# Another order of work around the paired down projections of a two-layer hybrid decoder

## The chip, the cores and the metric

One core of a Trainium2 chip runs the whole kernel in one launch. The metric is the device time of that launch in microseconds. The engines are TensorE (PE in the profile, with its weight loads as PEld), VectorE (DVE), ScalarE (ACT), GpSimd (POOL) and SyncE (SP, which only issues transfers here).

## What is computed

A decoder trunk of two layers over 1024 positions of width 1024, in float32. Each layer adds a mixer (attention heads and a short convolution) and then a gated feed-forward network; the change is in the latter:

```python
def conv_glu_ffn(h, w_up, conv_w, w_down):
    gu = h @ w_up
    g, u = jnp.split(gu, 2, axis=-1)
    g = causal_dwconv(g, conv_w)          # three taps per channel
    return (jax.nn.silu(g) * u) @ w_down  # D_FF = 2816 hidden channels

for layer in range(DEPTH):
    ...
    hn = rms_norm(h, norm_ffn_g[layer])
    h = h + conv_glu_ffn(hn, w_up[layer], conv_ffn_w[layer], w_down[layer])
```

## The kernel before

The residual h lies in SBUF as 8 rows of 128 channels by 1024 positions. The 2816 hidden channels are 22 tiles of 128, f = 0 to 21. Every matmul is made of three passes over float32 values split in a high and a low part (w_hi with hi, w_hi with lo, w_lo with hi), each 128 x 128 by 512 columns.

**Products.** One tile's gates and ups are made from seven block products in place of eight, with sums of quarters of the input (B11, B21, B22, and T1 to T4) and sums of quarters of the weights (A11, A12, A22, and S1 to S4). A product is 12 matmuls into one of four banks, in the order of STEADY: A11 with B11 into bank 0, A22 with T4 into 1, S1 with T1 into 2, S2 with T2 into 3, S3 with T3 into 0, A12 with B21 into 3, S4 with B22 into 2. VectorE puts the products together (`combine`: seven operations named `add_product`), and then adds two taps of the convolution to k_next (`convolve_gates`, one `scalar_tensor_tensor` of 128x1024 each), of which ScalarE has written the middle tap (`center`). ScalarE takes silu and VectorE multiplies by the ups (`value`); the result, k_next, is the tile's hidden value.

**Down projection.** The tiles are taken in pairs; pair p holds the values of tiles 2p and 2p+1. Its down projection is made of seven block products too, each of four rows of 3 matmuls (`down_row`): part one (PART_A) runs A11 with B11 into the four CHAINED banks 4 to 7 and S1 with T1 into the four SINGLE banks 0, 1, 3, 2, as soon as the even tile's value is there. Part two (PART_B) runs S2 with T2 into the CHAINED banks (on top of what is there), A12 with B21 into the SINGLE ones, S3 with T3 into the CHAINED ones, S4 with B22 into the SINGLE ones and A22 with T4 into the CHAINED ones. After each group VectorE adds its four rows into h (`add_row`, 128x512 from a bank), and TensorE may write a bank again only when VectorE has read it. `feed_forward` gives the order for all engines: up 0, up 1, then for each pair of the first ten: part one, up 2p+2, part two, up 2p+3; the last pair is done apart.

Here B21, T2 and so on stand for quarters of the pair's hidden values; GpSimd forms T1 to T4 from them (`form_t1`, `form_t2_t3`, `form_t4`), ScalarE rounds their high parts (`round_formed`) and GpSimd makes the low parts (`rest_t1` and so on).

**Weights.** SyncE loads blocks of 128x512 into a ring; ScalarE rounds each to w_hi (`round_blocks`, L1802) once the block four places before it has been used, and GpSimd makes w_lo (`later_weights`, `rest_of_block`, L759).

**Order.** Each engine's order is written out by hand; semaphores count events. add_done counts VectorE's adds into h, down_done TensorE's down rows, combined the sums of products, value_ready the hidden values, conv_ready the finished taps. In part two TensorE waits, before S3 with T3, for the adds of S2 with T2:

```python
                for m, b in enumerate(CHAINED):
                    pe.wait_ge(add_done, here + m + 1)
                    down_row(s3, "T3", m, b, False)
```

and before the first product of the next even tile, for the adds that read bank 0 in part one.

Of the kernel before, what the change touches and what calls it, by code (L numbers as in the profile page):

```python
# [10 lines left out]
SEQ = 1024  # L11
# [68 lines left out]
PART_A = (("A11", "B11"), ("S1", "T1"))  # L80
PART_B = (("S2", "T2"), ("A12", "B21"), ("S3", "T3"), ("S4", "B22"), ("A22", "T4"))

# [185 lines left out]
def build(nc, x_t, positions, stream, vectors, first_g, rope, identity, causal, dilation, out_t):  # L268
# [9 lines left out]
    with ctx:  # L278
# [180 lines left out]
        final_hi, final_lo = sem("final_hi"), sem("final_lo")  # L459
        penultimate_hi, penultimate_lo = sem("penultimate_hi"), sem("penultimate_lo")  # L460
        last_silu, last_value, last_hi, last_lo = sem("last_silu"), sem("last_value"), sem("last_hi"), sem("last_lo")
        value_ready, hi_ready, mix_ready = sem("value_ready"), sem("hi_ready"), sem("mix_ready")
# [244 lines left out]
        def _(pool):  # L707
# [218 lines left out]
            for layer in range(DEPTH):  # L926
# [17 lines left out]
                for what, n in feed_forward():  # L944
                    pair = (n - 1) // 2
                    if what == "down":
                        later_weights(4)
                    elif what == "part_a":
                        if n == 0:
                            later_weights(1)  # L950
                            form_t1(layer, 0)
                            later_weights(1)
                            rest_t1(layer, 0)
                        else:
                            later_weights(2)
                    elif what == "part_b":
                        rest_t2(layer, n)
                        rest_t4(layer, n)
                        later_weights(4)
                    elif n == 0:  # L960

                        first_weights(layer)
                    elif n > 1 and n % 2 == 0:
                        later_weights(PRODUCTS - 1)
                        form_t2_t3(layer, pair)
                        later_weights(1)
                        form_t4(layer, pair)
                        rest_t3(layer, pair)
                        later_weights(1)
                    elif n > 1:  # L970
                        later_weights(PRODUCTS - 1)
                        if n < F_TILES - 1:
                            form_t1(layer, (n - 1) // 2)
                        later_weights(1)
                        if n < F_TILES - 1:
                            rest_t1(layer, (n - 1) // 2)
# [6 lines left out]
        def _(pe):  # L983
# [118 lines left out]
            def products(layer, f):  # L1102
# [3 lines left out]
                for _, x, b in STEADY:  # L1106
# [6 lines left out]
                    elif f % 2 == 0:  # L1113
                        pe.wait_ge(add_done, added + 1 + 2 * (SINGLE.index(b) + 1))
                    else:
# [27 lines left out]
            def part_b(layer, pair):  # L1143
                added, done = layer * ADDS + pair * PAIR_ADDS, layer * (PAIRS - 1) + pair
                here = added + PART_A_ADDS
                s2, a12, s3, s4, a22 = (next_block() for _ in range(5))
                pe.wait_ge(block_ready, s2 + 1)
                pe.wait_ge(t_rested, 4 * done + 3)
                for m, b in enumerate(CHAINED):
                    pe.wait_ge(add_done, added + (1 + 2 * ROWS + m if m else 1))  # L1150
                    down_row(s2, "T2", m, b, False)
                pe.wait_ge(block_ready, a12 + 1)
                pe.wait_ge(b2_rested, done + 1)
                for m, b in enumerate(SINGLE):
                    pe.wait_ge(combined, PRODUCTS * (layer * F_TILES + 2 * pair + 2) + UP_ADDED[m])
                    down_row(a12, "B21", m, b, True)
                pe.wait_ge(block_ready, s3 + 1)
                for m, b in enumerate(CHAINED):
                    pe.wait_ge(add_done, here + m + 1)
                    down_row(s3, "T3", m, b, False)  # L1160
                pe.wait_ge(block_ready, s4 + 1)
                for m, b in enumerate(SINGLE):
                    pe.wait_ge(add_done, here + ROWS + m + 1)
                    down_row(s4, "B22", m, b, True)
# [375 lines left out]
        def _(act):  # L1540
# [37 lines left out]
            def prepare_ffn(layer):  # L1578
# [58 lines left out]
                keep_first_product(layer, 1)  # L1637
                act.activation(k_next[:, :], k_next[:, :], ACT.Silu).then_inc(silu_done, 1)

# [164 lines left out]
            def center(layer, f):  # L1804
# [3 lines left out]
                elif f % 2:  # L1808
                    act.wait_ge(b1_rested, done + 1)
                    act.wait_ge(t_formed, 4 * done + 1)  # L1810
                elif f:
# [42 lines left out]
            def hidden(layer, f):  # L1854
# [10 lines left out]
                elif f % 2 == 0:  # L1865
                    round_blocks(2)
                    keep_value(f - 1, mix_hi[0], layer * DOWNS + pair * PAIR_DOWNS + PART_A_DOWNS)
# [44 lines left out]
            for layer in range(DEPTH):  # L1912
# [4 lines left out]
                for what, n in feed_forward():  # L1917
                    if what == "up":
                        hidden(layer, n)
                    elif what == "part_a":  # L1920
                        if n == 0:
                            round_blocks(2)
                            silu()
                        else:
                            silu()
                            round_blocks(2)
                    elif what == "part_b":
# [9 lines left out]
        def _(dve):  # L1937
# [36 lines left out]

            def add_part_a():

                dve.wait_ge(down_done, downs[0] + 1)
                add_row(0, CHAINED[0], 0, 0, False)
                for m, b in enumerate(SINGLE):
                    dve.wait_ge(down_done, downs[0] + ROWS + m + 1)  # L1980
                    add_row(m, b, ROWS, 1, False)
                    add_row(m, b, 0, 1, True)
                for m, b in enumerate(CHAINED[1:], 1):
                    add_row(m, b, 0, 0, False)
                downs[0] += PART_A_DOWNS

            def add_part_b():
                add_rows(CHAINED, (0, 1, False))
                add_rows(SINGLE, (0, 0, False))
                add_rows(CHAINED, (ROWS, 1, True))  # L1990
# [293 lines left out]
            def first_blocks(layer):  # L2284
# [76 lines left out]
                sums[0] += PRODUCTS  # L2361
                value()

                add_product(layer, 1, 2, padded[:, PAD:PAD + HALF], 1, q_next[:, 0:HALF], first_kept)
                form("T4", 2, "T2", "B21", ALU.subtract)
                form("T4", 3, "T2", "B21", ALU.subtract)
# [35 lines left out]
            def combine(layer, f):  # L2402
# [12 lines left out]
                if f < F_TILES - 1:  # L2415
                    add_product(layer, f, 7, high_ups, 2, high_ups)
                    convolve_gates(layer, f)
                    dve.sem_inc(conv_ready, 1)
                else:
# [4 lines left out]
            def convolve_gates(layer, f):  # L2424
                dve.wait_ge(gate_used, seen(gate_used))
                for back in (1, 2):
                    tap = gain_of(layer, V_CONV_FFN + TAPS * f, TAPS - 1 - back)
                    dve.scalar_tensor_tensor(k_next[:, :], padded[:, PAD - back:PAD - back + SEQ], tap,  # L2428
                                             k_next[:, :], ALU.mult, ALU.add).then_inc(dve_seq, 1)
                    dve.wait_ge(dve_seq, seen(dve_seq))  # L2430

# [22 lines left out]
            def feed(layer):  # L2454

                for what, n in feed_forward():
# [7 lines left out]
                    elif what == "part_a":  # L2464
                        add_part_a()
                        if n == 0:
                            convolve_gates(layer, 1)
                            dve.sem_inc(conv_ready, 1)
                        value()
# [220 lines left out]
```

## Time and profile before

| | |
|---|---|
| median of 3 runs | 2454.46 us (2451.39 to 2456.73) |
| profiled execution | 2455.77 us |
| its span | 2453.8 us, 32218 instructions |
| mean granted TensorE clock | 0.993 |
| TensorE matmul busy | 2363.8 us (96%) |
| VectorE, ScalarE, GpSimd busy | 1674.6, 991.9, 1298.5 us |

The span is the time from the first to the last instruction of the profiled execution. Busy shares are of the span. Matmuls overlap in the pipe, so each is listed as longer than the step to the next. Idle time stands in brackets behind the row that ends it, with what ended it.

### The profile page before, as it was taken

What the parts mean: (1) busy time and instruction counts of PE and PEld (TensorE: products, weight loads), DVE (VectorE), ACT (ScalarE), POOL (GpSimd) and SP (SyncE); (2) the same over time, 40 slices, a digit from 0 to 9 for tenths busy, and PEclk for the clock granted to TensorE, in tenths of its full rate; (3) what the DMA queues carried; (4) which work ended last, traced back from release to release, by engine and by line L of the source; (5) the groups of instructions that cost most, each with busy time, mean ns of one, the idle gap of its engine ahead of it and who ended that gap; (6) DMA issues with size and microseconds to landing.
All of it is one profiled execution on the core that took longest, in us unless ns stands there. A gap on an engine that the chain in (4) does not pass through costs nothing.

```text
span 2453.8 us, 32218 instructions
## 1 busy us (share of the span) xinstructions
PE 2363.8 (96%) x11340; PEld 1955.7 (80%) x11340; DVE 1674.6 (68%) x2645; ACT 991.9 (40%) x1900; POOL 1298.5 (53%) x893
## 2 busy tenths in 40 slices
PE   7999999999999999999999999999999999999998
PEld 6888888777788788888878888878777888878886
DVE  8644777738667776666795557785486666777776
ACT  4344444525333333433523344444253343343333
POOL 3222323447666666777542223243577777767665
PEclk9999999999999999999999999999999999999999
DMA  9956786421333333333398658742213333333332
GB/s 287 227 139 162 194 205 130 115 60 39 91 99 93 92 97 94 95 93 95 127 283 203 163 148 210 186 100 81 60 58 93 95 91 95 95 95 98 97 95 81
DMA packets 162766, 304.45 MB, mean 124 GB/s; under 512 B 11440, under 2 KB 31024, under 8 KB 162608
## 3 DMA queue, kind: packets, MB, share of 16 engines
q1 hardware_dynamic: 129408, 238.20, 30.9%
q0 software_dynamic: 31616, 62.92, 14.3%
q8 instruction: 92, 1.51, 0.2%
q10 hardware_dynamic: 1584, 1.28, 0.2%
q14 instruction: 66, 0.54, 0.1%
HBM read 292.66 MB, written 135.27 MB: 174 GB/s over the span
## 4 chain that ended last, share of the span: by engine, by line
PE 75%; DVE 15%; issue 3%; POOL 3%; ACT 3%; DMA 1%; DVEq 0%; POOLq 0%; SPq 0%; ACTq 0%
PE ps L1045 11%; PE ps L1046 11%; PE ps L1047 11%; PE ps L1016 7%; PE ps L1018 7%; PE ps L1017 7%; PE ps L1123 4%; PE ps L1124 4%; PE ps L1125 4%; PE ps L1360 3%; DVE k_next L2428 3%; PE ps L1347 2%; DVE h L2071 1%; PE ps L1334 1%; PE ps L1335 1%
## 5 line engine op out<-in xcount | busy, mean ns | idle before, releaser
L759 POOL TENSOR_TENSOR w_lo<-more_stage,w_hi 128x512 fp32r<-128x512 f32 x304 | 445.7, 1466 | 225.1 <-ACT w_hi L1802 213.2
L724 POOL CAST w_hi<-stage 128x1024 fp32r<-128x1024 f32 x68 | 73.3, 1078 | 682.0 <-PE ps L1018 611.2
L1016 PE MATMUL ps<-x_hi,w_hi 128*128 128x512 f32 x928 | 376.5, 406 | 7.7 <-DVE q_next L1943 4.8
L1018 PE MATMUL ps<-x_hi,w_lo 128*128 128x512 f32 x928 | 365.1, 393 | 0.0
L1017 PE MATMUL ps<-x_lo,w_hi 128*128 128x512 f32 x928 | 364.6, 393 | 0.0
L1802 ACT ACTIVATE w_hi<-more_stage 128x512 fp32r<-128x512 f32 x294 | 181.5, 626 | 313.4 <-PE ps L1047 228.4
L1045 PE MATMUL ps<-T_hi,w_hi 128*128 128x512 f32 x688 | 268.3, 390 | 5.2 <-DVE q_next L2399 4.1
L1047 PE MATMUL ps<-T_hi,w_lo 128*128 128x512 f32 x688 | 267.7, 389 | 0.0
L1046 PE MATMUL ps<-T_lo,w_hi 128*128 128x512 f32 x688 | 267.7, 389 | 0.0
L759 POOL TENSOR_TENSOR w_lo<-stage,w_hi 128x512 fp32r<-128x512 f32 x146 | 197.2, 1351 | 132.1 <-ACT w_hi L1802 125.3
L1966 DVE TENSOR_TENSOR h<-ps,h 128x512 f32<-128x512 f32 x400 | 252.2, 683 | 11.1 <-PE ps L1125 5.2
L1045 PE MATMUL ps<-B_hi,w_hi 128*128 128x512 f32 x552 | 218.4, 396 | 16.3 <-DVE h L1964 15.6
L1046 PE MATMUL ps<-B_lo,w_hi 128*128 128x512 f32 x552 | 215.2, 390 | 0.0
L1047 PE MATMUL ps<-B_hi,w_lo 128*128 128x512 f32 x552 | 214.9, 389 | 0.0
L1016 PEld LDWEIGHTS ps<-x_hi,w_hi 128*128 128x128 f32 x928 | 176.3, 190 | 45.8 <-issue 8.2
L1018 PEld LDWEIGHTS ps<-x_hi,w_lo 128*128 128x128 f32 x928 | 176.0, 190 | 38.6
L1017 PEld LDWEIGHTS ps<-x_lo,w_hi 128*128 128x128 f32 x928 | 176.6, 190 | 35.6 <-issue 1.5
L1723 ACT ACTIVATE prob<-prob,neg_top 128x128 f32<-128x128 f32 (+3 forms) x192 | 147.4, 772 | 130.9 <-DVE neg_top L2111 130.5
L1123 PE MATMUL ps<-mix,w_hi 128*128 128x512 f32 x480 | 190.3, 396 | 9.3 <-issue 8.2
L1124 PE MATMUL ps<-mix,w_hi 128*128 128x512 f32 x480 | 188.1, 392 | 0.0
L1125 PE MATMUL ps<-mix,w_lo 128*128 128x512 f32 x480 | 188.0, 392 | 0.0
L726 POOL TENSOR_TENSOR w_lo<-stage,w_hi 128x1024 fp32r<-128x1024 f32 x68 | 168.9, 2484 | 5.5
(279 smaller groups left out, 4927.4 us busy)
## 6 DMA issues: line engine op xcount, KB each, us to landing
summed<-stream SPq DMA_DIRECT2D x40, 1024.0 KB, 10.4
more_stage<-stream SPq DMA_DIRECT2D x128, 256.0 KB, 2.6
stage<-stream SPq DMA_DIRECT2D x52, 512.0 KB, 3.6
more_stage<-summed SPq DMA_DIRECT2D x100, 256.0 KB, 2.6
summed_downs<-stream SPq DMA_DIRECT2D x16, 1280.0 KB, 10.8
summed<-stream POOLq DMA_DIRECT2D x20, 1024.0 KB, 15.0
summed<-summed POOLq DMA_DIRECT2D x20, 1024.0 KB, 13.0
more_stage<-summed_downs SPq DMA_DIRECT2D x60, 256.0 KB, 2.6
```

What stands on the lines that cost most here:

```text
L759: pool.tensor_tensor(block_of(w_lo, n), raw, block_of(w_hi, n).bitcast(f32), ALU.subtract)\
L1016: pe.matmul(out, w_hi[:, s, w], hi, start=start, stop=False)
L1017: pe.matmul(out, w_hi[:, s, w], lo, start=False, stop=False)
L1018: return pe.matmul(out, w_lo[:, s, w], hi, start=False, stop=stop)
L1045: pe.matmul(out, block_of(w_hi, n)[:, columns], hi, start=start, stop=False)
L1046: pe.matmul(out, block_of(w_hi, n)[:, columns], lo, start=False, stop=False)
L1047: return pe.matmul(out, block_of(w_lo, n)[:, columns], hi, start=False, stop=stop)
L1123: pe.matmul(bank(b), block_of(w_hi, n)[:, columns], hi, start=start, stop=False, skip_group_check=True)
L1124: pe.matmul(bank(b), block_of(w_hi, n)[:, columns], lo, start=False, stop=False, skip_group_check=True)
L1125: pe.matmul(bank(b), block_of(w_lo, n)[:, columns], hi, start=False, stop=True, skip_group_check=True)\
L1802: act.activation(block_of(w_hi, at), raw_block(layer, n), ACT.Copy).then_inc(block_hi, 1)
L1966: dve.tensor_tensor(row, bank(b), row, ALU.add).then_inc(add_done, 1)
```

## The change

The order of work on four engines is changed; no operation on data is added or left out but for the first tile's silu and value, which are now done in two halves each.

- TensorE: part two of each pair runs A12 with B21 first and S2 with T2 second. The waits count accordingly.
- VectorE, part one: the adds of S1 with T1 come first and those of A11 with B11 last. For pairs 1 to 9 the two taps of tile 2p+1 no longer stand ahead of the adds: the first tap, the two adds of bank 0, the second tap, then the others. For pair 0 the taps come between the adds of S1 with T1 and those of A11 with B11.
- VectorE, part two: the adds of B21's rows (SINGLE) come ahead of those of T2's (CHAINED).
- ScalarE: in part one, two roundings of weights (four for pair 0) come ahead of silu. A wait for an earlier copy is added in `center`.
- GpSimd: for pair 0, T1 is formed ahead of two blocks of weights instead of between them.
- The first tile of a layer: silu and value in halves, with the first sum of the next tile's products between the value's halves.

```diff
-PART_B = (("S2", "T2"), ("A12", "B21"), ("S3", "T3"), ("S4", "B22"), ("A22", "T4"))
+PART_B = (("A12", "B21"), ("S2", "T2"), ("S3", "T3"), ("S4", "B22"), ("A22", "T4"))
...
                         if n == 0:
-                            later_weights(1)
                             form_t1(layer, 0)
                             later_weights(1)
                             rest_t1(layer, 0)
+                            later_weights(1)
...
-                        pe.wait_ge(add_done, added + 1 + 2 * (SINGLE.index(b) + 1))
+                        pe.wait_ge(add_done, added + 2 * (SINGLE.index(b) + 1))
...
-                s2, a12, s3, s4, a22 = (next_block() for _ in range(5))
-                pe.wait_ge(block_ready, s2 + 1)
-                pe.wait_ge(t_rested, 4 * done + 3)
-                for m, b in enumerate(CHAINED):
-                    pe.wait_ge(add_done, added + (1 + 2 * ROWS + m if m else 1))
-                    down_row(s2, "T2", m, b, False)
+                a12, s2, s3, s4, a22 = (next_block() for _ in range(5))
                 pe.wait_ge(block_ready, a12 + 1)
                 pe.wait_ge(b2_rested, done + 1)
                 for m, b in enumerate(SINGLE):
                     pe.wait_ge(combined, PRODUCTS * (layer * F_TILES + 2 * pair + 2) + UP_ADDED[m])
                     down_row(a12, "B21", m, b, True)
+                pe.wait_ge(block_ready, s2 + 1)
+                pe.wait_ge(t_rested, 4 * done + 3)
+                for m, b in enumerate(CHAINED):
+                    pe.wait_ge(add_done, added + 2 * ROWS + m + 1)
+                    down_row(s2, "T2", m, b, False)
                 pe.wait_ge(block_ready, s3 + 1)
                 for m, b in enumerate(CHAINED):
-                    pe.wait_ge(add_done, here + m + 1)
+                    pe.wait_ge(add_done, here + ROWS + m + 1)
                     down_row(s3, "T3", m, b, False)
                 pe.wait_ge(block_ready, s4 + 1)
                 for m, b in enumerate(SINGLE):
-                    pe.wait_ge(add_done, here + ROWS + m + 1)
+                    pe.wait_ge(add_done, here + m + 1)
                     down_row(s4, "B22", m, b, True)
...
-                act.activation(k_next[:, :], k_next[:, :], ACT.Silu).then_inc(silu_done, 1)
+                for t in halves_of_t:
+                    act.activation(k_next[:, t], k_next[:, t], ACT.Silu).then_inc(first_silu, 1)
...
                     act.wait_ge(b1_rested, done + 1)
+                    act.wait_ge(b12_kept, done + 1)
                     act.wait_ge(t_formed, 4 * done + 1)
...
                 elif f % 2 == 0:
-                    round_blocks(2)
+                    if f > 2:
+                        round_blocks(2)
...
                     elif what == "part_a":
-                        if n == 0:
-                            round_blocks(2)
-                            silu()
-                        else:
-                            silu()
-                            round_blocks(2)
+                        round_blocks(4 if n == 0 else 2)
+                        silu()
...
-            def add_part_a():
-
-                dve.wait_ge(down_done, downs[0] + 1)
-                add_row(0, CHAINED[0], 0, 0, False)
-                for m, b in enumerate(SINGLE):
+            def add_part_a(layer, pair):
+
+                def add_shared(m):
                     dve.wait_ge(down_done, downs[0] + ROWS + m + 1)
-                    add_row(m, b, ROWS, 1, False)
-                    add_row(m, b, 0, 1, True)
-                for m, b in enumerate(CHAINED[1:], 1):
+                    add_row(m, SINGLE[m], ROWS, 1, False)
+                    add_row(m, SINGLE[m], 0, 1, True)
+
+                f = 2 * pair + 1
+                if pair:
+                    dve.wait_ge(gate_used, seen(gate_used))
+                    tap(layer, f, 1)
+                    add_shared(0)
+                    tap(layer, f, 2)
+                    dve.sem_inc(conv_ready, 1)
+                    for m in range(1, ROWS):
+                        add_shared(m)
+                else:
+                    for m in range(ROWS):
+                        add_shared(m)
+                    convolve_gates(layer, f)
+                    dve.sem_inc(conv_ready, 1)
+                for m, b in enumerate(CHAINED):
                     add_row(m, b, 0, 0, False)
                 downs[0] += PART_A_DOWNS
 
             def add_part_b():
+                add_rows(SINGLE, (0, 0, False))
                 add_rows(CHAINED, (0, 1, False))
-                add_rows(SINGLE, (0, 0, False))
                 add_rows(CHAINED, (ROWS, 1, True))
...
-                value()
-
+                low_t, high_t = halves_of_t
+                dve.wait_ge(first_silu, 2 * layer + 1)
+                dve.tensor_tensor(k_next[:, low_t], k_next[:, low_t], q_next[:, low_t], ALU.mult).then_inc(first_value, 1)
+                dve.wait_ge(first_value, 2 * layer + 1)
                 add_product(layer, 1, 2, padded[:, PAD:PAD + HALF], 1, q_next[:, 0:HALF], first_kept)
+                dve.wait_ge(first_silu, 2 * (layer + 1))
+                dve.tensor_tensor(k_next[:, high_t], k_next[:, high_t], q_next[:, high_t], ALU.mult).then_inc(first_value, 1)
+                dve.wait_ge(first_value, 2 * (layer + 1))
+                dve.sem_inc(value_ready, 1)
...
                 if f < F_TILES - 1:
                     add_product(layer, f, 7, high_ups, 2, high_ups)
-                    convolve_gates(layer, f)
-                    dve.sem_inc(conv_ready, 1)
+                    if f % 2 == 0:
+                        convolve_gates(layer, f)
+                        dve.sem_inc(conv_ready, 1)
```

`tap` is the one `scalar_tensor_tensor` of `convolve_gates`, which now calls it twice.

## Rows read from the trace of the kernel before

**Rows 1.** The page: busy time by engine, and the granted clock in 40 slices.

```profile
PE 2363.8 (96%) x11340; PEld 1955.7 (80%) x11340; DVE 1674.6 (68%) x2645; ACT 991.9 (40%) x1900; POOL 1298.5 (53%) x893
...
PEclk9999999999999999999999999999999999999999
```

**Rows 2.** Waits of TensorE's weight loads: for whom, us in total, times, longest.

```profile
PEld ps L1045 <- DVE h L1964: 23.2, 18, 1.3
...
PEld ps L1123 <- issue: 18.0, 22, 2.7
```

**Rows 3.** Windows: one pair's stretch, its length and each engine's busy time.

```profile
852.20:910.80 58.60, 57.67 (x254) 47.13 (x253) 40.55 (x55) 22.94 (x35) 40.71 (x30) 1.00 0.32 95
```

**Rows 4.** Timeline of TensorE, part one's last matmuls and the next product's first.

```profile
855.95 0.39 PE L1124 MATMUL ps<-mix,w_hi 128*128 128x512 f32 x1
856.18 0.39 PE L1125 MATMUL ps<-mix,w_lo 128*128 128x512 f32 x1
857.44 0.50 PE L1045 MATMUL ps<-B_hi,w_hi 128*128 128x512 f32 x1 [0.87 <-DVE h L1964]
857.77 0.39 PE L1046 MATMUL ps<-B_lo,w_hi 128*128 128x512 f32 x1
```

**Rows 5.** Timeline of VectorE in the same stretch.

```profile
851.85 3.51 DVE L2428 SCALAR_TENSOR_TENSOR k_next<-padded,vec,k_next 128x1024 f32<-128x1024 f32 x2
855.50 1.29 DVE L1966 TENSOR_TENSOR h<-ps,h 128x512 f32<-128x512 f32 x2
856.70 0.68 DVE L1964 TENSOR_TENSOR h<-h,ps 128x512 f32<-128x512 f32 x1
```

**Rows 6.** Timeline of TensorE in part two, from B21's last matmul to T3's.

```profile
881.83 0.39 PE L1125 MATMUL ps<-mix,w_lo 128*128 128x512 f32 x1
882.28 0.47 PE L1123 MATMUL ps<-mix,w_hi 128*128 128x512 f32 x1
882.59 0.40 PE L1124 MATMUL ps<-mix,w_hi 128*128 128x512 f32 x1
```

**Rows 7.** Timeline of VectorE in part two: the taps, then the first eight adds.

```profile
877.49 3.80 DVE L2428 SCALAR_TENSOR_TENSOR k_next<-padded,vec,k_next 128x1024 f32<-128x1024 f32 x2
881.44 4.87 DVE L1966 TENSOR_TENSOR h<-ps,h 128x512 f32<-128x512 f32 x8
```

**Rows 8.** Timeline of TensorE at the entry of layer one's feed-forward.

```profile
601.78 0.39 PE L1047 MATMUL ps<-T_hi,w_lo 128*128 128x512 f32 x1
604.23 0.50 PE L1045 MATMUL ps<-T_hi,w_hi 128*128 128x512 f32 x1 [2.06 <-DVE q_next L2399]
...
607.44 0.47 PE L1045 MATMUL ps<-T_hi,w_hi 128*128 128x512 f32 x1 [0.20 <-DVE T_lo L2307]
...
614.94 0.47 PE L1123 MATMUL ps<-mix,w_hi 128*128 128x512 f32 x1 [1.76 <-issue]
...
640.60 0.77 PE L1123 MATMUL ps<-mix,w_hi 128*128 128x512 f32 x1 [2.33 <-issue]
...
645.86 0.40 PE L1123 MATMUL ps<-mix,w_hi 128*128 128x512 f32 x1
```

**Rows 9.** Timeline of GpSimd beside the taps ahead of part two.

```profile
876.69 1.30 POOL L759 TENSOR_TENSOR w_lo<-stage,w_hi 128x512 fp32r<-128x512 f32 x1
878.16 2.05 POOL L759 TENSOR_TENSOR w_lo<-stage,w_hi 128x512 fp32r<-128x512 f32 x1 [0.18 <-POOL w_lo L759]
```

**Rows 10.** Timeline of GpSimd and VectorE around the first tile's value.

```profile
600.89 1.30 POOL L759 TENSOR_TENSOR w_lo<-more_stage,w_hi 128x512 fp32r<-128x512 f32 x1
...
601.47 1.80 DVE L2435 TENSOR_TENSOR k_next<-k_next,q_next 128x1024 f32<-128x1024 f32 x1 [1.67 <-ACT k_next L1638]
```

**Rows 11.** TensorE behind two gaps, and windows of a us with the granted clock.

```profile
79.81 0.47 PE L1016 MATMUL ps<-x_hi,w_hi 128*128 128x512 f32 x1 [2.10 <-DVE q_next L1943]
...
1286.25 0.77 PE L1016 MATMUL ps<-x_hi,w_hi 128*128 128x512 f32 x1 [2.68 <-DVE q_next L1943]
...
641.00:642.00 1.00, 1.00 (x3) 0.74 (x3) 0.96 (x2) 0.00 (x0) 1.00 (x1) 0.50 0.14 51
```

More of the change, by code:

```diff
@@ L460, in build @@
         penultimate_hi, penultimate_lo = sem("penultimate_hi"), sem("penultimate_lo")
+        first_silu, first_value = sem("first_silu"), sem("first_value")
         last_silu, last_value, last_hi, last_lo = sem("last_silu"), sem("last_value"), sem("last_hi"), sem("last_lo")
@@ L2426, in convolve_gates, with tap @@
                 for back in (1, 2):
[L2427 to L2430, printed above, removed]
+                    tap(layer, f, back)
+            def tap(layer, f, back):
+                by = gain_of(layer, V_CONV_FFN + TAPS * f, TAPS - 1 - back)
+                dve.scalar_tensor_tensor(k_next[:, :], padded[:, PAD - back:PAD - back + SEQ], by,
+                                         k_next[:, :], ALU.mult, ALU.add).then_inc(dve_seq, 1)
+                dve.wait_ge(dve_seq, seen(dve_seq))
             def value():
@@ L2464, in feed @@
                     elif what == "part_a":
[L2465 to L2468, printed above, removed]
+                        add_part_a(layer, n)
                         value()
```

## The prediction, made before the changed kernel ran

> **What bounds the kernel now.** I read the page's shares first. TensorE is busy for 2363.8 of 2453.8 us and its granted clock is at full speed in nearly every slice [rows 1]; so the time is TensorE's own work plus whatever holds it up. I then asked for its waits [rows 2]. Two of them repeat in the feed-forward loop. One is the first product after part one of a down projection, 18 times (once for each of pairs 1 to 9 in two layers). The weight load waits 23.2 us in total for a VectorE subtraction into h. The other is a down row of part two, whose releaser the profile calls "issue", 22 times.
>
> The windows give the loop's period: 58.60 us for one pair [rows 3]. Steady matmuls follow each other every 0.227 us (855.95 to 856.18 in [rows 4]). A pair has 168 matmuls of products and 84 of down rows, so 252 x 0.2267 = 57.13 us, and 1.47 us of each pair is stall. Both places can be seen. In [rows 4] the step from 856.18 to 857.44 is 1.26 us, or 1.03 too long, and the slow step behind it adds 0.13: **stall A, 1.16 us**. In [rows 5] the cause is plain. VectorE first runs two taps of the convolution (3.51 us), then adds; the third add, the second that reads bank 0, starts at 856.70, lasts 0.68 and ends at 857.38. In [rows 6] the step from 881.83 to 882.28 is 0.22 too long, with 0.08 behind it: **stall B, about 0.31 us**. Down row 1 of T3 waits there for the first add of part two, which begins at 881.44, right behind two taps of 3.80 us [rows 7]. Eight adds take 4.87 us, so they start 0.597 us apart.
>
> The entry to the feed-forward loop is looser [rows 8]. Between the last matmul before the first gap (601.78) and the 148th after it (645.86; 2 x 12 of products, 24 of part one, 84 of products, 16 of part two) lie 44.08 us instead of 148 x 0.2267 = 33.55: 10.5 us lost per layer, in gaps of 2.06, 0.20, 1.76 and 2.33 us, three small ones, and a slow clock at the end.
>
> **The change, part by part.** *Part one's adds (removes stall A).* VectorE will run tap one, the two adds that read bank 0, tap two, then the other shared adds. Row 1 of S1*T1 is complete 15 matmuls into part one, at 854.14 + 0.39 = 854.53 (the matmul lengths of [rows 4]). With the 0.11 us that the engine shows elsewhere, the two adds run from 854.64 to 855.92. TensorE wants bank 0's weights at about 856.2. Stall A goes: **18 x 1.16 = -20.9 us**. The next product wants bank 1 at 858.9. Tap two starts near 855.9; at 1.2 us alone, bank 1 is free at 858.4, and at 2.2 us (the slow tap) at 859.4. I take 0, with 0.5 per pair as the upper bound. The value product comes some 0.5 to 1.3 us later than before; it is needed by the copy of the first product, which frees bank 0 for the fifth one, 48 matmuls (10.9 us) on. I find 0.2 us of slack and keep another 0.3 per pair above it.
>
> *ScalarE's order.* Two roundings ahead of silu instead of behind it, and a wait for a copy made long before. Nothing is queued behind that TensorE wants within the next block. Cost 0; if it fails, the block that is late stands four blocks (10.9 us) ahead.
>
> *Part two's order (enlarges stall B).* This is the main term. Before, TensorE wrote T2's rows to the four chained banks, B21's to the four single ones, and came back to the chained banks with T3. The adds followed that order, so T3's first row waited for **add one**. Now B21's rows come first, T2's second, T3's third, all adds in the same order: T3's first row needs T2's row added, which is **add five**, and VectorE does not start adding earlier, since both taps still stand ahead in every even tile. TensorE reaches T3 after 24 matmuls either way. So the wait grows by four adds: 4 x 0.597 = 2.39 us, from 0.31 to 2.70. The gap proper would be 2.4 us: add five ends at 881.44 + 2.39 + 0.69 = 884.52, the previous matmul at 882.22. The other three rows need no wait, since rows take 0.68 us and adds 0.60. What the new order gives, T2's operands wanted 2.7 us later, is worth nothing in a steady pair, where no wait for them is left. **18 x 2.39 = +43.0 us** for pairs 1 to 9.
>
> What can move this term is the tap pair ahead of the adds. A tap is 1.2 us when alone. GpSimd works without a pause there, and its operations stretch from 1.30 to 2.05 us [rows 9] while the taps stretch too, so the two engines take turns. With GpSimd always queued, two taps cost 1.1 + 1.1 + 1.1 us plus what is left of the operation found running (0 to 1.3): 3.4 to 4.6. Before it was 3.80. I keep 3.8 with -0.4 and +0.8 per pair as bounds.
>
> *The entry to the loop.* The first tile's value is split in halves. The whole one began at 601.47 and took 1.80 us because GpSimd was in an operation of 1.30 us from 600.89 [rows 10]; the half will begin at 601.0, still wait until 602.19, and end near 602.75, so product T1 starts at 603.55 instead of 604.23. The second half and T4's remainders then come later; I get T4's product at 608.4 instead of 607.44. GpSimd forms T1 first, 4 us earlier, so S1*T1 starts without its 1.76 us gap at 613.9 instead of 614.94. The small gaps and the gap of 2.33 us ahead of part two go (four roundings now stand ahead of silu, and GpSimd stands idle no more), and stall B of 2.7 appears here as well. Loss per layer: 1.6 + 2.1 + 2.7 = 6.4 instead of 10.5, **2 x -4.1 = -8.2 us**, bounds -14 and 0.
>
> *The clock.* A gap of 2.4 us, twenty times, has a price of its own. In this trace TensorE's clock fell from 2.4 to 1.2 GHz (granted 0.50 [rows 11]) around gaps of 2.10 us at 79.81, 2.33 at 640.60 and 2.68 at 1286.25 [rows 8, 11], and around two more of 2.23 and 2.31: all five of 2.10 us and longer. It didn't fall around the gaps of 2.06 and 1.76 in [rows 8]. A fall costs about seven matmuls at 0.427 instead of 0.227 us, 1.4 to 1.6 us. Since 2.06 and 2.10 differ in outcome, length alone doesn't decide; I take a fall in 12 of 20 stalls: **12 x 1.5 = +18.0 us**, bounds 0 and +30. The Trainium skill ("TensorE: Matmul & The Clock Gate", section "HAM oscillation — how this bites in real kernels") would let gaps of this length pass without a fall; by it this term is 0 and the forecast 2468. The five falls speak against that here.
>
> Sum: -20.9 + 43.0 - 8.2 + 18.0 = **+31.9 us**. The profiled execution took 2455.77 us (span 2453.8); the median shown is 1.3 lower, so 2454.46 + 31.9 = **2486 us**.
>
> **The rivals.**
> - *Stall B as large, but the clock stays up.* 2454.5 + 13.9 = 2468 us. For it: gaps of 2.06 passed. Against: five of five longer ones did not.
> - *Every gap costs a fall and the taps meet GpSimd badly.* Clock +30, taps or the bounds at the other products +8: 2454.5 + 13.9 + 30 + 8 = 2506 us.
> - *The other side: the taps run free.* If GpSimd's work has moved out of the way of the tap pair ahead of part two, the taps take 2.4 instead of 3.8 us and the adds start 1.4 us earlier. Stall B is 1.3, no fall of the clock follows from so short a gap, and the sum is -20.9 + 18 x 1.0 - 8.2 - 2 x 1.4 = -13.9: 2441 us. It decides where stall B is below about 1.9 us, so tap pairs below 3.0. For it: part one's pair of taps in pair 0 took little over 2.4 us with GpSimd idle. Against: GpSimd's chain from value_ready keeps its distance to TensorE, and it is busy throughout this stretch [rows 9].
> - *The stall is hidden.* T3's wait could cost nothing if TensorE had arrived late anyway, as at 640.60. That was pair 0 alone; in steady pairs it arrives early enough to have waited for add one already [rows 6]. This gives 2454.5 - 20.9 - 13 = 2420 us, and I give it 3 in 100.
>
> **How the numbers follow.** Stall B with part of the falls 0.48, without falls 0.22, with all of them and more 0.15, taps free 0.12 (some of it within 0.2% of before), hidden 0.03. The predicted time is the first's, 2486. The range reaches from 2458, below the case without falls with its entry gains at their bound, to 2508. That leaves out the two fast cases and a tail above. A change under 0.2% (about 5 us) can't be told from none. Faster 0.13, same 0.04, slower 0.83.
>
> **What would show it.** In the profile after: a wait of TensorE at the down row's line, some 20 times near 2.4 us, where L1123 now shows 18 of under half a microsecond; its previous matmul is the last of T2; the wait at L1045 for the subtraction into h gone; the period of a pair 59.8 us with the clock up and 61.3 with a fall; granted clock near 0.98 instead of 0.993 over the span; taps ahead of part two at 3.4 to 4.6 us, and the fifth add ending just before TensorE resumes. The prediction is wrong if the adds into the chained banks end before TensorE has done B21's and T2's 24 matmuls, so if stall B is under 1.9 us, or if a new wait stands at the second or the fifth product of an even tile.

## The result, and the profile after

The changed kernel takes 2470.93 us (median of 4 runs, 2468.4 to 2473.64), the kernel before 2453.32 us beside it: +17.6 us, a ratio of 1.007 with a 95% interval of 1.0053 to 1.0088. Slower was forecast, at 2486 us in a range of 2458 to 2508.

The page of the changed kernel, its engines' busy time and the granted clock, to be read against [rows 1]:

```profile
PE 2357.2 (96%) x11340; PEld 1952.4 (79%) x11340; DVE 1683.9 (68%) x2647; ACT 989.8 (40%) x1902; POOL 1318.1 (53%) x893
...
PEclk9999999999999999999999999999999999999999
```

The mean granted clock of this execution is 0.996; it was 0.993 before, and 0.98 was forecast. TensorE is no more busy than before; what grew is its idle time. Its longest waits in the feed-forward part (for whom, us in total, times, longest), here those of the matmuls, where [rows 2] has those of the weight loads:

```profile
PE ps L1124 <- DVE h L1966: 26.8, 20, 1.3
PE ps L1124 <- POOLq L763: 16.6, 20, 1.1
```

The wait at a product for the subtraction into h, 18 times before, is gone. Two others stand at the down rows, each 20 times. The timeline of TensorE in part two of the same pair as in [rows 6] shows where they are:

```profile
875.22 0.39 PE L1126 MATMUL ps<-mix,w_lo 128*128 128x512 f32 x1
876.42 0.50 PE L1124 MATMUL ps<-mix,w_hi 128*128 128x512 f32 x1 [0.82 <-POOLq L763]
...
879.05 0.39 PE L1126 MATMUL ps<-mix,w_lo 128*128 128x512 f32 x1
880.78 0.47 PE L1124 MATMUL ps<-mix,w_hi 128*128 128x512 f32 x1 [1.34 <-DVE h L1966]
```

The first is ahead of T2's first row, behind B21's twelve matmuls; the second is ahead of T3's. VectorE in the same stretch, parts one and two, as in [rows 5, 7]:

```profile
849.12 1.27 DVE L2452 SCALAR_TENSOR_TENSOR k_next<-padded,vec,k_next 128x1024 f32<-128x1024 f32 x1
851.91 0.69 DVE L1966 TENSOR_TENSOR h<-ps,h 128x512 f32<-128x512 f32 x1 [1.52 <-PE ps L1126]
852.52 0.68 DVE L1964 TENSOR_TENSOR h<-h,ps 128x512 f32<-128x512 f32 x1
853.12 1.28 DVE L2452 SCALAR_TENSOR_TENSOR k_next<-padded,vec,k_next 128x1024 f32<-128x1024 f32 x1
...
860.53 1.94 DVE L2459 TENSOR_TENSOR k_next<-k_next,q_next 128x1024 f32<-128x1024 f32 x1
...
873.60 3.80 DVE L2452 SCALAR_TENSOR_TENSOR k_next<-padded,vec,k_next 128x1024 f32<-128x1024 f32 x2
877.55 4.88 DVE L1966 TENSOR_TENSOR h<-ps,h 128x512 f32<-128x512 f32 x8
```

The fifth of the eight adds ends at 877.55 + 4 x 0.597 + 0.69 = 880.63, and TensorE resumes at 880.78. The two taps ahead of them take 3.80 us, as before. The taps of part one, now apart, take 1.27 and 1.28.

GpSimd in the same stretch: the low parts of T2 and T4 (L835) come first, and only then the block that TensorE waits for, whose operation is itself stretched from 1.30 to 2.25 us beside the taps:

```profile
871.57 1.29 POOL L835 TENSOR_TENSOR mix<-mix_raw,mix 128x512 fp32r<-128x512 f32 x1 [0.18 <-POOL w_lo L760]
872.81 1.29 POOL L835 TENSOR_TENSOR t_lo<-t_raw,t_hi 128x512 fp32r<-128x512 f32 x1
874.07 2.25 POOL L760 TENSOR_TENSOR w_lo<-stage,w_hi 128x512 fp32r<-128x512 f32 x1
```

It ends at 876.32, and T2's first row starts at 876.42.

For what follows, the starts of part one, products and part two in TensorE's timeline are compared. All times are us; the loss is the length less 0.2267 for each matmul.

| stretch (matmuls) | before | loss | after | loss |
|---|---|---|---|---|
| a steady pair, part one (24) | 850.97 to 857.44 | 1.03 | 848.24 to 853.68 | 0.00 |
| products of the even tile (84) | to 876.61 | 0.13 | to 872.72 | 0.00 |
| part two (60) | to 890.54 | 0.33 | to 889.04 | 2.72 |
| products of the odd tile (84) | to 909.58 | 0.00 | to 908.08 | 0.00 |
| pairs 1 to 9, from the first product of tile 3 to the last of tile 21, layers one and two | 546.7, 546.7 | | 557.6, 557.6 | |
| entry, from the first product to the first of tile 3, layers one and two | 92.0, 92.0 | | 89.5, 91.1 | |

The steady pairs cost 10.9 us more in each layer, 21.8 in all, and the entry 2.5 and 0.9 us less: +18.3 us in the feed-forward, beside +17.6 in the medians. The spans of the two profiled executions differ by only 12.8 us (they took 2455.77 and 2468.40 us, one above its median and one below). The rest is outside the changed code. The first layer's feed-forward begins 3.9 us earlier in the trace after, and the stretch between the two feed-forwards is 2.9 us shorter: single executions differ in how long TensorE's clock is down there. The windows from 45 to 90 us show it for the start (length, busy times of PE, PEld, DVE, ACT, POOL, then the clock: 0.89 before and 0.96 after). First before, then after:

```profile
45.00:90.00 45.00, 41.98 (x185) 34.30 (x186) 37.90 (x81) 12.24 (x32) 12.99 (x9) 0.89 0.97 232
```

```profile
45.00:90.00 45.00, 42.43 (x201) 35.24 (x202) 40.15 (x82) 12.41 (x32) 15.27 (x10) 0.96 0.98 240
```

Between the feed-forwards, the gap of 2.68 us that had the clock down at 1286.25 [rows 11] is there again after, as long, and this time the matmuls behind it run at full speed (granted clock 1.00 from 1286 to 1296 us):

```profile
1290.74 0.47 PE L1017 MATMUL ps<-x_hi,w_hi 128*128 128x512 f32 x1 [2.68 <-DVE q_next L1943]
```

### The profile page after: what moved, and what is told of

The parts are those of the page before. It is cut to its first block, busy times and chain, and to the rows that moved or that the text cites. A ratio compares the mean times of both kernels' runs of the same rounds, so it can differ in the third digit from the quotient of the medians.

```text
span 2466.6 us, 32258 instructions
## 1 busy us (share of the span) xinstructions
PE 2357.2 (96%) x11340; PEld 1952.4 (79%) x11340; DVE 1683.9 (68%) x2647; ACT 989.8 (40%) x1902; POOL 1318.1 (53%) x893
## 3 DMA queue, kind: packets, MB, share of 16 engines
q10 hardware_dynamic: 1584, 1.28, 0.2%
## 4 chain that ended last, share of the span: by engine, by line
PE 73%; DVE 19%; issue 3%; ACT 3%; POOL 1%; DMA 1%; DVEq 0%; SPq 0%; POOLq 0%; ACTq 0%
PE ps L1046 11%; PE ps L1048 11%; PE ps L1047 11%; PE ps L1017 6%; PE ps L1019 6%; PE ps L1018 6%; PE ps L1124 4%; DVE k_next L2452 4%; PE ps L1125 4%; PE ps L1126 4%; PE ps L1361 3%; DVE h L1966 3%; PE ps L1348 2%; DVE h L2084 2%; PE ps L1335 1%
## 5 line engine op out<-in xcount | busy, mean ns | idle before, releaser
L760 POOL TENSOR_TENSOR w_lo<-stage,w_hi 128x512 fp32r<-128x512 f32 x146 | 214.4, 1468 | 122.7 <-ACT w_hi L1804 117.3
```

The lines of the kernel that those rows point to most:

```text
L760: pool.tensor_tensor(block_of(w_lo, n), raw, block_of(w_hi, n).bitcast(f32), ALU.subtract)\
```

## The experiments

Nine kernels ran, in three groups; each group has its own runs of the kernel before, and ratios are to them.

| run | median, us | ratio to before (95%) | steady period, us |
|---|---|---|---|
| before | 2453.0 to 2455.1 | | 58.6 |
| changed | 2470.9 | 1.007 (1.0053 to 1.0088) | 59.84 |
| part two's old order | 2442.7 | 0.9956 (0.9942 to 0.9971) | 58.28 |
| adds of T2 first | 2442.1 | 0.9956 (0.9941 to 0.9971) | 58.23 |
| new order alone, on before | 2507.4 | 1.0229 (1.0212 to 1.0246) | 61.0 or 62.5 |
| S2's block earlier | 2507.1 | 1.0221 (1.0206 to 1.0236) | 61.4 |
| both remedies | 2432.3 | 0.9914 (0.9899 to 0.9929) | 57.77 |
| and the first value whole | 2426.1 | 0.9889 (0.9872 to 0.9905) | 57.77 |
| two adds ahead | 2450.7 | 0.9981 (0.9971 to 0.9991) | 58.67 |
| and two blocks ahead of T4 | 2421.6 | 0.9866 (0.985 to 0.9882) | 57.47 |
| old order, first value whole | 2438.0 | 0.993 (0.9914 to 0.9945) | 58.27 |

**Part two's order put back.** The changed kernel with the old `part_b`, `add_part_b` and PART_B.

```diff
-PART_B = (("A12", "B21"), ("S2", "T2"), ("S3", "T3"), ("S4", "B22"), ("A22", "T4"))
+PART_B = (("S2", "T2"), ("A12", "B21"), ("S3", "T3"), ("S4", "B22"), ("A22", "T4"))
...
             def add_part_b():
-                add_rows(SINGLE, (0, 0, False))
                 add_rows(CHAINED, (0, 1, False))
+                add_rows(SINGLE, (0, 0, False))
```

> The changed kernel with part two's order alone put back: TensorE runs S2 with T2 first and A12 with B21 second, and VectorE adds in that order. Theory (the loss is part two's order, T3 waiting for the fifth add instead of the first; the other edits gain): a pair's part two loses about 0.3 us instead of the 2.72 seen in the changed kernel, the period falls from 59.84 to about 57.5 us, and the time is 2471 - 20 x 2.4 = about 2423 us. Rival (part one's new order and the earlier roundings cause the loss, part two's order is neutral): the time stays near 2471 us.

2442.7 us, 28 below the changed kernel: the loss is part two's order, and the rival is out. But the period is 58.28, not 57.5. TensorE waits twice more here:

```profile
754.71 0.47 PE L1124 MATMUL ps<-mix,w_hi 128*128 128x512 f32 x1
...
758.17 0.50 PE L1124 MATMUL ps<-mix,w_hi 128*128 128x512 f32 x1 [0.47 <-POOLq L763]
```

T2's first row starts 0.48 us behind the last product's matmul instead of 0.23 (GpSimd ends T2's low part only just before), and A12's block is 0.62 us late in its turn. With the slow steps behind them the two cost 0.32 and 0.73 us per pair. In the changed kernel the hidden value of the odd tile ends 10.3 us ahead of part two, before it was 12.7, and GpSimd ends T2's low part later by 1.3 us relative to part two. So T2 first, which waited for nothing in the kernel before, has a price in this one.

**T2's adds first.** TensorE keeps the new order; VectorE adds T2's rows ahead of B21's.

```diff
-                    pe.wait_ge(add_done, here + ROWS + m + 1)
+                    pe.wait_ge(add_done, here + m + 1)
                     down_row(s3, "T3", m, b, False)
...
-                    pe.wait_ge(add_done, here + m + 1)
+                    pe.wait_ge(add_done, here + ROWS + m + 1)
                     down_row(s4, "B22", m, b, True)
...
-                add_rows(SINGLE, (0, 0, False))
-                add_rows(CHAINED, (0, 1, False))
+                for m, b in enumerate(CHAINED):
+                    dve.wait_ge(down_done, downs[0] + ROWS + m + 1)
+                    add_row(m, b, 0, 1, False)
+                for m, b in enumerate(SINGLE):
+                    add_row(m, b, 0, 0, False)
+                downs[0] += 2 * ROWS
```

> The changed kernel, TensorE in its new order, but VectorE adds T2's four rows before B21's in part two, so that T3 waits for the first add again. Theory (the number of adds ahead of T3 makes the second gap; the first gap is S2's weight block): the gap of 1.34 us before T3 goes, the gap of 0.82 us before T2 stays, the period is about 58.1 us and the time about 2471 - 20 x 1.75 = 2436 us. Rival (T2's rows and T3's rows are now back to back, so T3 waits for VectorE whatever it adds first): under 10 us gained, 2461 us or more.

2442.1 us and a period of 58.23. The gap before T3 is gone; the one before T2 is what it was:

```profile
756.66 0.50 PE L1124 MATMUL ps<-mix,w_hi 128*128 128x512 f32 x1 [0.82 <-POOLq L763]
```

So the two gaps have two causes. T3's rows right behind T2's bring no gap here, and that rival is out. The time is 6 us above the expectation: the period fell by 1.61 us, not 1.75, and the entry has a slow clock that the changed kernel's profile shows in the second layer only (below, with the first value).

**The new order alone.** The kernel before with the changed kernel's `part_b`, `add_part_b` and PART_B, nothing else.

> The kernel before with part two's order alone changed (TensorE's rows and VectorE's adds). Theory: stall A of 1.16 us stays, stall B grows by 2.39 us in 20 parts: at least 2453 + 48 = 2501 us with TensorE's clock up. Here GpSimd has S2's block ready before TensorE asks for it, since TensorE is 1.16 us later, so stall B should be one gap of about 2.4 us instead of two of 0.8 and 1.3, and the clock should fall in many pairs: up to 2453 + 48 + 30 = 2531 us. If the clock does not fall around single gaps of 2.4 us: 2501 us and a mean granted clock as before. Rival (the order is neutral): 2453 us.

2507.4 us, +54. Here the wait before T3 is one gap, and the same gap has two outcomes. The timeline of TensorE at two of them:

```profile
706.74 0.47 PE L1123 MATMUL ps<-mix,w_hi 128*128 128x512 f32 x1 [2.47 <-DVE h L1966]
...
767.78 0.76 PE L1123 MATMUL ps<-mix,w_hi 128*128 128x512 f32 x1 [2.47 <-DVE h L1966]
```

Windows of 3 us behind each, with granted clocks of 1.00 and 0.54:

```profile
707.00:710.00 3.00, 3.00 (x14) 2.45 (x14) 3.00 (x6) 0.16 (x1) 0.86 (x1) 1.00 0.51 160
768.00:771.00 3.00, 3.00 (x8) 2.38 (x9) 2.40 (x5) 0.00 (x0) 0.89 (x1) 0.54 0.56 156
```

Of the 18 steady pairs, 6 have part two at 17.7 to 17.9 us and 12 at 16.3 us: the clock fell around six of 18 equal gaps, and a fall costs about 1.4 us here. Pair 0's gap is 2.87 us in layer one and 2.89 in layer two, and there it is a weight block that ends it. The clock stayed up behind the first (granted 1.00 from 643 to 646 us) and fell behind the second:

```profile
642.90 0.50 PE L1123 MATMUL ps<-mix,w_hi 128*128 128x512 f32 x1 [2.87 <-POOLq L762]
```

**S2's block earlier.** The changed kernel with one GpSimd edit.

```diff
                         rest_t2(layer, n)
+                        later_weights(1)
                         rest_t4(layer, n)
-                        later_weights(4)
+                        later_weights(3)
```

> The changed kernel with one GpSimd edit: in part two the low part of S2's weight block is made before T4's low part instead of behind it, about 1.25 us earlier. Theory (the fifth add sets when T3 may start, whatever happened before): the gap of 0.82 us before T2 goes and the gap before T3 grows from 1.34 to about 2.3 us; the period stays 59.8 us where the clock holds, so no gain (2471 us), and up to 30 us lost where it falls around the now unbroken gap. Rival (the weight block is a cost of its own): 20 x 0.95 gained, 2452 us.

2507.1 us: the remedy for one wait, taken alone, makes the kernel 36 us slower. The gap before T2 is gone; the one before T3 has taken its time up and is unbroken, and TensorE runs at 1.2 GHz behind it:

```profile
764.60 0.39 PE L1127 MATMUL ps<-mix,w_lo 128*128 128x512 f32 x1
767.47 0.77 PE L1125 MATMUL ps<-mix,w_hi 128*128 128x512 f32 x1 [2.48 <-DVE h L1967]
768.03 0.63 PE L1126 MATMUL ps<-mix,w_hi 128*128 128x512 f32 x1
```

The window behind it, with a granted clock of 0.55:

```profile
768.00:771.00 3.00, 3.00 (x9) 2.37 (x8) 2.40 (x4) 0.00 (x0) 1.43 (x2) 0.55 0.68 186
```

In all 20 pairs part two takes 17.7 to 18.2 us, where the changed kernel takes 16.3 in a steady one; the gaps are 2.47 or 2.48 us, 2.25 in one pair and 2.73 and 2.74 in pair 0. With the gap in two pieces the clock stayed up in 20 of 20 pairs, with the gap whole it fell in 20 of 20. So it was the stall before T2 that kept the clock up in the changed kernel: it cut the gap in two.

**Both remedies.** T2's adds first, and S2's block ahead of T4's low part.

> TensorE in the changed kernel's order, with both of the edits tried one by one before: VectorE adds T2's rows ahead of B21's, and GpSimd makes the low part of S2's block before T4's. Theory: the price of the new order lay in two waits that need two remedies. The 0.82 us gap before T2 goes; T3 waits at most 0.2 us for the first add; the clock stays up. The period falls from 58.23 us (adds alone mended) to about 57.4 us and the time to 2442 - 20 x 0.85 = about 2425 us. Rival (the earlier block brings the long gap and the slow clock by itself, as in the run that had it alone): 2442 us or more.

2432.3 us, 10 below the run with T2's adds first alone, but 7 short of the expectation. Period 57.77: the next block, S3's, is now the late one.

```profile
759.16 0.50 PE L1125 MATMUL ps<-mix,w_hi 128*128 128x512 f32 x1 [0.35 <-POOLq L763]
```

**The first value whole.** The kernel with both remedies, and the first tile's silu and value as they were before.

```diff
-                for t in halves_of_t:
-                    act.activation(k_next[:, t], k_next[:, t], ACT.Silu).then_inc(first_silu, 1)
+                act.activation(k_next[:, :], k_next[:, :], ACT.Silu).then_inc(silu_done, 1)
...
```

VectorE's two multiplications become one `value()` again in the same way.

> The kernel with both remedies, but the first tile's silu and value whole again, as in the kernel before. In the changed kernel the stretch from the first product of the feed-forward to the first down row is 47.2 and 48.9 us, before it was 46.2 in both layers. Theory (the halves cost there: the second half waits for GpSimd and delays T4's low parts, a gap of 1.9 us where the clock may fall): 1 to 2.5 us per layer gained, 2 to 5 in all against the run with both remedies, and the second layer's stretch back at about 46.2 to 46.5. Rival (the halves gain, since T1's product starts 0.7 us earlier in each layer): 1 to 3 us slower.

2426.1 us, 6.2 below. The stretch from the first product to the first down row is 46.2 us in both layers again, where it was 48.8 and 47.2. In the changed kernel's entry the gaps are (timeline of TensorE, both layers):

```profile
599.67 0.50 PE L1046 MATMUL ps<-T_hi,w_hi 128*128 128x512 f32 x1 [1.32 <-DVE q_next L2418]
...
604.66 0.47 PE L1046 MATMUL ps<-T_hi,w_hi 128*128 128x512 f32 x1 [1.93 <-DVE T_lo L2320]
...
1817.79 0.62 PE L1046 MATMUL ps<-T_hi,w_hi 128*128 128x512 f32 x1 [1.99 <-DVE T_lo L2320]
1818.20 0.63 PE L1047 MATMUL ps<-T_lo,w_hi 128*128 128x512 f32 x1
```

The halves shorten the gap before product T1 from 2.06 to 1.32 us and open one of 1.9 to 2.0 before T4. Behind that gap the clock was down in the second layer (the matmuls of 0.63 us), and of the six profiles of kernels with the halves, two layers each, ten of twelve show it. That is the 2.6 us per layer with a fall, and 1.0 without. These stretches hold 3.7 of the 6.2 us; part of the rest is a clock that was down for 6.8 us between the feed-forwards in the profile with the halves and not in this one. With the value whole the gap before T1 is 1.99 to 2.07 us again, and the clock fell there in 3 of 10 layers (five profiles, that of before included). So the slightly shorter gap before T4 brought more falls than the longer one before T1.

**Two adds ahead.** The kernel with S2's block earlier, two of B21's adds ahead of T2's and two behind.

```diff
-                add_rows(SINGLE, (0, 0, False))
-                add_rows(CHAINED, (0, 1, False))
+                for m, b in enumerate(SINGLE[:2]):
+                    ...
+                for m, b in enumerate(CHAINED):
+                    ...
+                for m, b in enumerate(SINGLE[2:], 2):
+                    ...
```

TensorE's waits count accordingly.

> The changed kernel with S2's block made early, and two of B21's four adds ahead of T2's instead of four (the other two behind). Theory (each add ahead of T2's costs T3 one step of 0.597 us, in the gap and nowhere else): the gap before T3 is 2.48 - 1.19 = 1.29 us, too short for a fall of the clock; the period is 61.41 - 1.19 - 1.57 (the clock) = 58.65 us, and the time 2507 - 20 x 2.76 = about 2452 us. Rival (the wait is for T2's rows or weights rather than for the adds): the gap stays at or near 2.48 us and the time near 2507 us.

2450.7 us, period 58.67. Two steps of 0.597 us less make the gap 2.48 - 1.19 = 1.29, and no pair has the clock down:

```profile
761.33 0.47 PE L1125 MATMUL ps<-mix,w_hi 128*128 128x512 f32 x1 [1.28 <-DVE h L1967]
```

**Two blocks ahead of T4's low part.** The best kernel so far, with `later_weights(2)`, `rest_t4`, `later_weights(2)`.

> The kernel with both remedies and the whole first value, with one more GpSimd edit: two blocks' low parts (S2's and S3's) are made before T4's instead of one. In the run before, TensorE's only wait in a steady pair was 0.35 us of idle, 0.52 us too long a step in all, before T3, for S3's block; the period was 57.8 us. Theory (each product of part two needs its own block in turn, T4's low part only at the end): that wait goes, the first add sets T3's start with at most 0.2 us, the period is 57.2 to 57.4 us and the time 2426 - 20 x 0.5 = about 2416 us. Rival (T4's low part or a later block is late instead): no gain, 2426 us or more.

2421.6 us, 4.5 below the run before it, against 10 expected; its period is 57.47 where 57.13 would be no loss at all. No wait for a weight block is left in a steady pair. What is left, 0.34 us per pair, is T3's wait for the first add, as in the kernel before; the profile shows it as a wait of the weight load of at most 0.7 us, "issue" as in [rows 2]:

```profile
PEld ps L1125 <- issue: 9.7, 20, 0.7
```

This is the fastest version: 1.3% below the kernel before.

**The old order with the first value whole.** The changed kernel with part two's old order and the whole first value; GpSimd makes T4's low part ahead of all four blocks, as in the changed kernel.

> The changed kernel with part two's old order (S2 with T2 first) and the whole first value: what the other edits give by themselves. Theory (with the old order the changed kernel waits 0.24 us for T2's low part and 0.62 us for A12's block in each pair, since GpSimd forms T2 later; and the halves cost 6 us wherever they are): 2443 - 6 = about 2437 us, periods as in the run with the old order alone, 58.28 us. Rival (the 6 us of the halves came from the new order's entry): 2443 us. Against the best version with B21 first it shows what that order is worth once its waits are mended: about 20 us.

2438.0 us, as expected. Against the version before it, 2421.6 us, the difference is 16 us. That is not what B21 first is worth, though the expectation says so: the two versions differ in the GpSimd edit too. TensorE still waits for A12's block here, and with the slow step behind it this costs 0.76 us per pair, 15 of the 16 us:

```profile
PEld ps L1124 <- POOLq L763: 18.3, 20, 0.9
```

The old order with two blocks made ahead of T4's low part did not run. An estimate from these rows: without the wait for the block only T2's 0.32 us per pair would be left, where B21 first leaves 0.34 at T3. So by the estimate the two orders come out equal, and that the new one gains anything is not shown.

## Why the prediction was right, and where it was not

The forecast held in sign and range; of its four terms two were nearly exact and two too large. The two errors have opposite signs: the clock made the forecast 18.0 us too long, the entry 4.8 us too short.

1. *Stall A, -20.9 us: right.* Part one and the products behind it lose 0.00 instead of 1.03 + 0.13 us in a steady pair. The two adds of bank 0 start at 851.91, 0.11 us behind the end of the row (848.24 + 14 x 0.2267 + 0.39 = 851.80), as worked out; the tap behind them took 1.28 us, the short one of the two cases. (A tap alone takes 1.27 or 1.28 us in the traces and a pair 2.59, so the forecast's 1.2 and 2.4 are a little low; no term of the sum rests on them.)
2. *Stall B, +43.0 us: the sum right, the mechanism half told.* The loss in part two went from 0.33 to 2.72 us; 0.31 and 2.70 were forecast. That T3 waits for add five is shown by moving the adds: none of B21's ahead, no gap for an add; two ahead, 1.28; four, 2.48. But the forecast gave the whole loss to one gap of 2.4 us. In the changed kernel 0.82 of it falls before T2, to a weight block that GpSimd makes behind the low parts of T2 and T4. Since T3's start is set by VectorE in either case, this second wait cost nothing by itself. The forecast's sign of about 20 waits near 2.4 us therefore did not appear.
3. *The clock, +18.0 us: the term that failed.* The step was "I take a fall in 12 of 20 stalls". There was none in any of the 20 pairs, as the gap came in pieces of 0.82 and 1.34 us. Where the gap is whole the price was well sized: a period of 61.4 instead of 59.84 us with S2's block earlier, 1.6 us per fall, and 1.4 in the other kernel. The share of 12 in 20 is neither of those measured: 7 of 20 in one kernel and 20 of 20 in the other, pair 0 included. Nor does its ground hold, that all five gaps of 2.10 us and longer brought a fall: in the changed kernel's own trace one of 2.68 us passed. Without this term the forecast reads 2468 us, and the measured median is 2470.9.
4. *The entry, -8.2 us: right in sign, too large.* -2.5 and -0.9 us were measured. The gaps at T1's and T4's products came as forecast (3.7 us lost in the first layer). What was left out: a gap of 0.57 and 0.90 us before the fifth product, 0.2 us at part one in the first layer, 0.2 to 0.3 more in part two, and the slow clock behind the gap at T4's product. The run with the whole value shows that one edit of the entry, the halves, was a loss: without it that kernel is 6.2 us faster, and the entry's stretch up to part one 1.0 to 2.6 us shorter per layer.

One premise of the forecast failed. It took it that no wait for T2's operands is left in a steady pair, so that wanting them later is worth nothing. In this kernel, where value ends later, the old order does wait for T2's low part, 0.32 us per pair; whether the new order gains by it is open, as said above.

The forecast's 0.2 us of slack at the second and fifth products was enough in steady pairs. But the late value is what made GpSimd late further on, by the order of work in the two traces; no run moved the value. VectorE's product took 1.94 us, where it had taken 1.22 (the row below, from before). GpSimd was within an operation when it began (860.09 to 861.39, the product from 860.53). The forecast followed the late value to the fifth product, and no further.

```profile
862.68 1.22 DVE L2435 TENSOR_TENSOR k_next<-k_next,q_next 128x1024 f32<-128x1024 f32 x1
```

The rival of the clock staying up is thus what happened in time, though not for its reason: not that the chip lets such a gap pass, but that there was no such gap. The rule of the Trainium skill ("TensorE: Matmul & The Clock Gate", section "HAM oscillation — how this bites in real kernels"), by which gaps of this length pass, does not hold here: 27 of 40 unbroken gaps of 2.25 to 2.89 us in two kernels had the clock down behind them.

Open: why 7 of 20 gaps brought a fall in one kernel and all 20 in the other. The length is not the reason: 2.47 us did both, 2.87 passed and 2.25 did not. Also not tried is a version in which T2's adds are first and the taps come behind them.

## What to carry to other kernels

When the order of producers on TensorE is changed, count for each bank what now stands on VectorE's queue between its last write and its next one: here two products into the same banks became neighbours, and the adds of a third stood between. Mend waits that lie one behind the other together: against the changed kernel, one edit alone gained 29 us, the other lost 36, since it joined two gaps into one, and both gained 39. Splitting an operation to start its reader earlier has to be weighed against what the second half delays: here the product that reads the first half started 0.7 us earlier, and the product behind it waited 1.9 us instead of 0.2. And to compare two orders, give both the same remedies.

## What the runs showed of the hardware

- TensorE's granted clock fell from 1.00 to 0.50 behind unbroken gaps of 2.25 to 2.89 us in 27 of 40 pairs of two kernels, and in none of the changed kernel's 20 pairs, whose gaps of 0.55 to 1.05 and 1.30 to 1.34 us have twelve matmuls between them. At the entry it fell in ten of twelve layers behind a gap of 1.91 to 1.99 us before T4's product, and in 3 of 10 behind one of 1.99 to 2.07 us before T1's. The length alone does not decide: gaps of 2.68 and 2.87 us passed.
- A fall cost 1.4 to 1.6 us each time: five to eight matmuls at about 0.427 instead of 0.227 us.
- A tap that began while GpSimd was idle or between operations took 1.27 or 1.28 us. The pair of taps ahead of part two, begun within GpSimd's operations, took 3.79 to 3.83 us in 17 or 18 of the 18 steady pairs of each of the eleven kernels. A GpSimd operation that took 1.30 us undisturbed took 2.25 beside them. The second tap of the pair shown above began at 875.22 within a GpSimd operation that ended at 876.32, and ended 1.08 us behind it. The Trainium skill ("SBUF — State Buffer", section "Who interferes with whom") says that a VectorE instruction with two SBUF inputs contends with a GpSimd one that reads SBUF, and that the lock on their shared ports is exclusive; these rows agree.
